# A two-block model on one core: the MLP's down product kept feature-major, and its up product in chunks of 256 columns

## Chip, core and metric

The kernel runs on one core of a Trainium2 chip. The metric is the device time of one execution in microseconds (us), lower is better; for the kernel before, three executions were timed.

## What is computed

Two model blocks run one after the other on 256 tokens of width 1024, in float32: a gated linear attention and a differential attention, each followed by an MLP, then a mixing block of three branches, a cross attention and a third MLP. The change touches the three MLPs, which are all alike:

```python
def rms_norm(x, g):
    y = x * rsqrt(mean(x * x, axis=-1) + EPS)
    return y * g
def sqrelu_mlp(xn, w1, w2):             # xn (256, 1024), w1 (1024, 4096), w2 (4096, 1024)
    return square(relu(xn @ w1)) @ w2
h = h + sqrelu_mlp(rms_norm(h, mlp_norm[layer]), mlp_w1[layer], mlp_w2[layer])
```

## The kernel before, in words

All weights (220 MB) are cut on the host into 420 chunks of 1024 x 128 numbers. Two chunks make a slab of 1 MB, and SyncE streams the 210 slabs through a ring of four buffers, `raw`. Float32 accuracy comes from splitting: ScalarE casts a chunk to `w_hi` (fp32r, `cut_hi`, L959), VectorE subtracts to get `w_lo` (bf16, `cut_lo`, L1505), and both run AHEAD = 3 chunks ahead of TensorE over four slots. The other operand is split the same way into `X.hi`, `X.lo` and `X.bf` (`operand` on ScalarE, L965 to L969; `operand_lo` on VectorE, L1518 and L1520); there are two such sets, XA and XB. Each chunk costs hi x hi, hi x lo and lo x bf.

Most chunks go through `chunk` (L373 to L389). The activations are kept feature-major: 128 features on the partitions, 256 tokens in the free dimension. For each of eight k, the 128x128 square of weights is stationary, and `X.hi` (L382) and `X.lo` (L383) move through, 256 columns each; then eight matmuls of 256 columns take `w_lo` with `X.bf` (L388). All 24 add into one half bank of PSUM; chunks take banks 0 to 3 in turn, and `bank_free` counts the banks given back.

The MLP (`mlp`, one function on each engine) has its own two forms. It works in four hidden groups of 1024; a group is 8 up chunks and 8 down chunks, and the two middle groups are turns of a loop.

- `up_chunk` (L414): `X.hi` and `X.lo` lie beside each other, so one matmul of 512 columns (L422) takes both, eight of them to a whole bank, then eight of 256 columns for the low part (L427). VectorE adds the two halves of the bank (TENSOR_REDUCE, L1574), GpSimd takes max(x, 0) (L2133) and squares it (L2135), and the result is split into XB.
- `down_chunk` (L432): here the activations are stationary and the weights move. A chunk holds two k and four column squares; for each k and each half of the tokens there are two matmuls of 512 columns (L441, L442) and later one for the low part (L451). The sums stand token-major in banks 4 to 7 (`down_sums(t, b)`, token half t, column half b) over all four groups.

Since the norm's factor 1/rms belongs to a token and relu squared is homogeneous of degree two, the MLP multiplies by 1/rms squared at the very end (`rtok2`, one number per token, from `rms_tok`). `stats` has TensorE add up GpSimd's sums of squares (L464 as a row of 256 tokens, L467 as a column); it stands after the first chunk of each stage.

At the end of the last group the sums must be turned. ScalarE copies and scales banks 4 and 5 to SBUF (`to_sbuf`, L1017) after down chunk 3, TensorE transposes 8 squares after down chunk 4 (`turn(0)`, L491), and VectorE adds them to H (`final`, L1558, two feature blocks of 256 at a time: a pair). After the last down chunk the same comes again for banks 6 and 7: one copy by ScalarE, one by VectorE (L1590), `turn(1)`, two adds. Each `final` lets ScalarE build the next stage's operand, VectorE its low part, GpSimd its squares (`sum_squares`, L2108 to L2115), and at last TensorE the next stage's chunk. Between these, ScalarE and VectorE have cuts to make, in the order in which the program is written:

```python
cut_hi(c + 8 + j + AHEAD, o + j + AHEAD)          # ScalarE, down chunk j
if last and X is not None and j in (5, 6):
    final(j - 5)
```

In this document MLP 0 is the one of the first attention block (from 178 us), MLP 1 the second (from 534 us), MLP 2 the last of the program (from 1441 us). Behind MLP 2 there are only the eight output DMAs (L1484), issued by ScalarE as the pairs of H are done.

Of the kernel before, what the change touches and what calls it, by code (L numbers as in the profile page):

```python
# [18 lines left out]
ALU = mybir.AluOpType  # L19
# [35 lines left out]
PAIR_ADDS = TAPS - 1  # L55
HN_K, HN_Q = 2 * DIFF_HEADS, 2 * DIFF_HEADS + 2
# [53 lines left out]
def program(nc, w_d, par_d, con_d, gm_d, x_d, mem_d, band_d, out_d):  # L110
    ctx = ExitStack()
    with ctx:
# [25 lines left out]
        rtok2 = sb("rtok2", [P, NT])  # L138
# [71 lines left out]
        m_sum, m_sq = cut(2, T), cut(2, T)  # L210
        m_tok = cut(NT, D)
# [77 lines left out]
        relu_done, sq_done = sem("relu_done"), sem("sq_done")  # L289
        hn_sq, hn_mm, hn_ln, hn_r, hn_out = [sem("hn_" + n) for n in ("sq", "mm", "ln", "r", "out")]  # L290
        tok_out, turned = sem("tok_out"), sem("turned")
# [25 lines left out]
        def down_sums(t, b):  # L317

            return ps[:, 4 + 2 * b + t, :]
# [50 lines left out]
        def _(pe):  # L370
# [43 lines left out]
            def up_chunk(c, j, build):  # L414

                s, bank = j % HI_SLOTS, j % BANKS
                pe.wait_ge(hi_done, c + 1)
                pe.wait_ge(bank_free, c - BANKS + 1)
                for k in range(KC):
                    if build is not None:  # L420
                        pe.wait_ge(XA.lo_done, KC * build + k + 1)
                    mm(ps[:, bank, :], w_hi[:, s, k], XA.both[:, k].rearrange("p a t -> p (a t)"), start=k == 0, stop=False)  # L422
                pe.wait_ge(lo_done, c + 1)
                for k in range(KC):
                    if build is not None:
                        pe.wait_ge(XA.bf_done, KC * build + k + 1)
                    last = mm(ps[:, bank, 0:T], w_lo[:, s, k], XA.bf[:, k], start=False, stop=k == KC - 1)  # L427
                last.then_inc(gemm_done, 1)

            def down_chunk(c, slot, j, build, first, last):  # L430

                s, b, a = slot % HI_SLOTS, j // 4, j % 4  # L432
                pe.wait_ge(hi_done, c + 1)
                for i in range(2):
                    k = 2 * a + i
                    cols = slice(4 * i, 4 * i + 4)
                    if b == 0:
                        pe.wait_ge(XB.lo_done, KC * build + k + 1)
                    for t in range(NT):
                        at = slice(t * P, (t + 1) * P)  # L440
                        mm(down_sums(t, b), XB.hi[:, k, at], w_hi[:, s, cols], start=first and k == 0, stop=False)  # L441
                        mm(down_sums(t, b), XB.lo[:, k, at], w_hi[:, s, cols], start=False, stop=False)  # L442
                pe.wait_ge(lo_done, c + 1)
                for i in range(2):
                    k = 2 * a + i
                    cols = slice(4 * i, 4 * i + 4)
                    if b == 0:
                        pe.wait_ge(XB.bf_done, KC * build + k + 1)
                    for t in range(NT):
                        at = slice(t * P, (t + 1) * P)  # L450
                        done = mm(down_sums(t, b), XB.bf[:, k, at], w_lo[:, s, cols], start=False, stop=last and k == KC - 1)  # L451
# [27 lines left out]
            def mlp(c0, m, x_build, xb_build0, nu):  # L479
# [3 lines left out]
                def turn(b):  # L483

                    for t in range(NT):
                        pe.wait_ge(tok_out, 4 * m + 2 * b + t + 1)
                    for pair in range(2 * b, 2 * b + 2):
                        for i in range(2):
                            n = 2 * pair + i
                            for t in range(NT):  # L490
                                last = nc.tensor.transpose(ps[:, pair, i * T + t * P:i * T + (t + 1) * P],  # L491
                                                           m_tok[:, t, n * P:(n + 1) * P], ident)
                        last.then_inc(turned, 1)
# [1835 lines left out]
```

## Time and profile before

| what | value |
|---|---|
| times of three executions | 1635.01, 1637.58, 1643.14 us |
| median | 1637.58 us |
| profiled execution, first to last instruction (span) | 1632.4 us |
| profiled execution's own time | not among the times shown |
| TensorE matmul busy | 1454.7 us, 89% |
| TensorE weight load busy | 1186.9 us, 73% |
| VectorE, ScalarE, GpSimd busy | 65%, 54%, 25% |
| mean granted TensorE clock | 0.949 of 2.4 GHz |

A profile row names a line of the kernel, the engine, the operation, and out<-in with the shapes. Matmuls are pipelined: the duration shown for one includes its way through the array, so rows are read by their starts. `x8` means that eight alike are merged, from the start of the first to the end of the last. An idle time in brackets stands before the instruction, with what ended it.

### The profile page before, as it was taken

Reading aid. Unit: us, or ns where it says so; the run is one execution under the profiler, and the core shown is the slowest. Engines: PE = TensorE matmul, PEld = TensorE weight load, DVE = VectorE, ACT = ScalarE, POOL = GpSimd, SP = SyncE. Lnnn points to the kernel's source line nnn. Section 1 sums busy time; section 2 is a strip of 40 time slices with the busy share of each in tenths; the row PEclk is TensorE's granted clock in tenths of the full one; section 3 lists DMA queues with packets and bytes.
Section 4 is the critical chain, followed back from the end, with each engine's and each line's share of the span. In section 5 each row is a group of like instructions: output and inputs, shape, how many; then the busy total and the mean of one; then the engine's idle time right before and its main releaser. Section 6 shows DMA issues by size and latency. Waiting matters only on the chain. (4 is left out here: it accounts for less than half of the span.)

```text
span 1632.4 us, 26380 instructions
## 1 busy us (share of the span) xinstructions
PE 1454.7 (89%) x9598; PEld 1186.9 (73%) x9622; DVE 1056.8 (65%) x1664; ACT 885.6 (54%) x1710; POOL 415.4 (25%) x429
## 2 busy tenths in 40 slices
PE   5987899998988899989978879898898799789998
PEld 5876777766866677769877767778786688577776
DVE  4794666665565666666999755567576665366665
ACT  4443545456455544456988655454565465454443
POOL 3000433341001433244987100004000012043332
PEclk9997999998997899999999999999999899999999
DMA  7330455552821455534444322225343343145551
GB/s 293 109 124 26 143 193 196 190 181 103 183 102 52 158 203 183 203 134 152 155 140 147 136 94 104 85 106 182 117 149 129 114 155 132 50 155 190 198 187 70
DMA packets 35304, 233.54 MB, mean 143 GB/s; under 512 B 3840, under 2 KB 6912, under 8 KB 7936
## 3 DMA queue, kind: packets, MB, share of 16 engines
q1 hardware_dynamic: 30816, 223.75, 38.0%
q10 hardware_dynamic: 3216, 4.19, 1.7%
q0 software_dynamic: 1168, 4.20, 0.9%
q8 instruction: 67, 1.10, 0.3%
q14 instruction: 37, 0.30, 0.1%
HBM read 227.93 MB, written 4.19 MB: 142 GB/s over the span
## 5 line engine op out<-in xcount | busy, mean ns | idle before, releaser
L1505 DVE TENSOR_TENSOR w_lo<-raw,w_hi 128x1024 bf16<-128x1024 f32 x420 | 537.5, 1282 | 286.6 <-ACT w_hi L959 282.9
L959 ACT CAST w_hi<-raw 128x1024 fp32r<-128x1024 f32 x420 | 436.4, 1043 | 239.2 <-PE ps L451 96.6
L382 PE MATMUL ps<-xa_both,w_hi 128*128 128x256 f32 x912 | 240.1, 302 | 30.6 <-ACT w_hi L959 11.8
L383 PE MATMUL ps<-xa_both,w_hi 128*128 128x256 f32 x912 | 225.7, 286 | 0.0
L422 PE MATMUL ps<-xa_both,w_hi 128*128 128x512 f32 x768 | 211.2, 415 | 13.4 <-DVE xa_both L1520 13.4
L382 PEld LDWEIGHTS ps<-xa_both,w_hi 128*128 128x128 f32 x912 | 179.6, 197 | 39.2 <-issue 15.7
L382 PE MATMUL ps<-xb_both,w_hi 128*128 128x256 f32 x704 | 189.1, 307 | 20.0 <-DVE xb_both L1518 11.0
L383 PEld LDWEIGHTS ps<-xa_both,w_hi 128*128 128x128 f32 x912 | 179.9, 197 | 0.4
L383 PE MATMUL ps<-xb_both,w_hi 128*128 128x256 f32 x704 | 175.8, 288 | 0.0
L422 PEld LDWEIGHTS ps<-xa_both,w_hi 128*128 128x128 f32 x768 | 140.8, 193 | 45.9 <-DVE xa_both L1520 17.0
L441 PE MATMUL ps<-w_hi,xb_both 128*128 128x512 f32 x384 | 167.1, 435 | 0.0
L382 PEld LDWEIGHTS ps<-xb_both,w_hi 128*128 128x128 f32 x704 | 139.6, 198 | 32.0 <-issue 18.9
L2133 POOL TENSOR_SCALAR arena<-arena 128x256 f32<-128x256 f32 x96 | 86.2, 897 | 292.3 <-DVE arena L1574 292.3
L442 PE MATMUL ps<-w_hi,xb_both 128*128 128x512 f32 x384 | 150.5, 392 | 0.0
L388 PE MATMUL ps<-xa_bf,w_lo 128*128 128x256 bf16 x912 | 123.1, 279 | 21.3 <-DVE w_lo L1505 21.3
L383 PEld LDWEIGHTS ps<-xb_both,w_hi 128*128 128x128 f32 x704 | 140.4, 199 | 0.4
L2162 POOL TENSOR_TENSOR arena<-arena 128x512 f32<-128x512 f32 x90 | 126.9, 1410 | 49.1 <-ACT arena L1219 38.4
L965 ACT CAST xb_both<-arena 128x256 fp32r<-128x256 f32 x152 | 61.4, 404 | 126.7 <-POOL arena L2135 119.4
L2108 POOL TENSOR_TENSOR sumsq<-H 128x256 f32<-128x256 f32 x7 | 4.3, 612 | 433.9 <-DVE H L1542 404.2
L388 PEld LDWEIGHTS ps<-xa_bf,w_lo 128*128 128x128 bf16 x912 | 81.8, 100 | 37.5 <-DVE w_lo L1505 24.6
L427 PE MATMUL ps<-xa_bf,w_lo 128*128 128x256 bf16 x768 | 103.2, 279 | 0.0
L451 PE MATMUL ps<-w_lo,xb_bf 128*128 128x512 bf16 x360 | 96.2, 381 | 1.4
(291 smaller groups left out, 2354.2 us busy)
## 6 DMA issues: line engine op xcount, KB each, us to landing
raw<-weights SPq DMA_DIRECT2D x210, 1024.0 KB, 4.8
band<-arena ACTq DMA_DIRECT2D x1, 3072.0 KB, 35.5
arena<-band POOLq DMA_DIRECT2D x8, 256.0 KB, 3.2
arena<-gla_masks SPq DMA_DIRECT2D x1, 1088.0 KB, 15.2
H<-x_t SPq DMA_DIRECT2D x1, 1024.0 KB, 4.9
arena<-mem_t POOLq DMA_DIRECT2D x1, 1024.0 KB, 5.2
arena<-band POOLq DMA_DIRECT2D x8, 128.0 KB, 2.7
out_t<-H ACTq DMA_DIRECT2D x8, 128.0 KB, 2.1
```

What stands on the lines that cost most here:

```text
L382: mm(ps[:, bank, 0:T], w_hi[:, s, k], X.hi[:, k], start=k == 0, stop=False)
L383: mm(ps[:, bank, 0:T], w_hi[:, s, k], X.lo[:, k], start=False, stop=False)
L388: last = mm(ps[:, bank, 0:T], w_lo[:, s, k], X.bf[:, k], start=False, stop=k == KC - 1)
L422: mm(ps[:, bank, :], w_hi[:, s, k], XA.both[:, k].rearrange("p a t -> p (a t)"), start=k == 0, stop=False)
L427: last = mm(ps[:, bank, 0:T], w_lo[:, s, k], XA.bf[:, k], start=False, stop=k == KC - 1)
L441: mm(down_sums(t, b), XB.hi[:, k, at], w_hi[:, s, cols], start=first and k == 0, stop=False)
L442: mm(down_sums(t, b), XB.lo[:, k, at], w_hi[:, s, cols], start=False, stop=False)
L451: done = mm(down_sums(t, b), XB.bf[:, k, at], w_lo[:, s, cols], start=False, stop=last and k == KC - 1)
L959: nc.scalar.copy(w_hi[:, j % HI_SLOTS].rearrange("p k n -> p (k n)"), raw[:, j // 2 % RING, j % 2]).then_inc(hi_done, 1)
L1505: TT(w_lo[:, j % HI_SLOTS].rearrange("p k n -> p (k n)"), raw[:, j // 2 % RING, j % 2], w_hi[:, j % HI_SLOTS].rearrange("p k n -> p (k n)" ...
L2133: G.tensor_scalar(m_sq[:, j % 2], m_sum[:, j % 2], 0.0, None, ALU.max).then_inc(relu_done, 1)
L2162: G.tensor_tensor(both, both, c_prod[:, a % PRODUCTS], ALU.add).then_inc(ca["add"], 1)
```

## The change

Both MLP forms become plain feature-major chunks. The up chunks go through `chunk` itself; VectorE's one instruction reads the 256 sums, takes max(x, 0) and multiplies by 1/rms per token (so `rstd` is needed before the first of them, and TensorE's `stats` makes the row in place of the column); GpSimd only squares. In the down chunk the weights are stationary and XB moves, 256 columns each; the eight sums (output blocks n) stand in the halves of banks 4 to 7. `DOWN` orders the squares: four chunks with two k and four n each for k 0 to 3, then four chunks that each finish the two n of a pair. So a pair is complete with down chunks 4, 5, 6 and 7 of the last group, and `final` adds it from PSUM directly. Copies, transposes and their buffers are gone. `bank_free` now counts two for a pair.

```diff
+DOWN = [[(k, n) for k in (j // 2 * 2, j // 2 * 2 + 1) for n in range(j % 2 * 4, j % 2 * 4 + 4)] for j in range(4)]
+DOWN += [[(k, n) for n in (2 * p, 2 * p + 1) for k in range(4, 8)] for p in range(4)]
...
+        def down_sums(n):
+            return ps[:, 4 + n // 2, n % 2 * T:(n % 2 + 1) * T]
+        def down_pair(p):
+            return ps[:, 4 + p, :].rearrange("p (n t) -> p n t", n=2)
...
             def down_chunk(c, slot, j, build, first, last):
-                s, b, a = slot % HI_SLOTS, j // 4, j % 4
+                s, ready = slot % HI_SLOTS, {0: (0, 1), 2: (2, 3), 4: (4, 5, 6, 7)}.get(j, ())
                 pe.wait_ge(hi_done, c + 1)
+                for i, (k, n) in enumerate(DOWN[j]):
+                    if k in ready and n == DOWN[j][0][1]:
+                        pe.wait_ge(XB.lo_done, KC * build + k + 1)
+                    opens = first and k == 0 and n % 2 == 0
+                    mm(down_sums(n), w_hi[:, s, i], XB.hi[:, k], start=opens, stop=False)
+                    mm(down_sums(n), w_hi[:, s, i], XB.lo[:, k], start=False, stop=False)
                 pe.wait_ge(lo_done, c + 1)
+                for i, (k, n) in enumerate(DOWN[j]):
+                    if k in ready and n == DOWN[j][0][1]:
                         pe.wait_ge(XB.bf_done, KC * build + k + 1)
+                    done = mm(down_sums(n), w_lo[:, s, i], XB.bf[:, k], ...)
                 done.then_inc(gemm_done, 1)
...
                     for j in range(8):
-                        up_chunk(c + j, o + j, x_build if first and j == 0 else None)
+                        chunk(c + j, o + j, XA, x_build if first and j == 0 else None)
                         if first and j == 0:
-                            stats(nu, False, True)
+                            stats(nu, True, False)
...
                         down_chunk(c + 8 + j, o + j, j, xb_build0 + g, first, last)
-                        if last and j == 4:
-                            turn(0)
-                    if last:
-                        turn(1)
...
                 def final(pair):                                   # ScalarE
-                    act.wait_ge(bank_free, c0 + 60 + pair + 1)
+                    act.wait_ge(bank_free, c0 + 56 + 2 * pair + 2)
...
                         if first and j == 0:
-                            rms_tok()
+                            rms(nu, rstd)
...
-                        if last and j == 4:
-                            act.wait_ge(gemm_done, c + 12)
-                            for t in range(NT):
-                                to_sbuf(t, 0)
                         cut_hi(c + 8 + j + AHEAD, o + j + AHEAD)
-                        if last and X is not None and j in (5, 6):
+                        if last and X is not None and j >= 5:
                             final(j - 5)
-                    if last:
-                        act.wait_ge(gemm_done, c + 16)
-                        to_sbuf(0, 1)
-                        if X is not None:
-                            final(2)
-                            final(3)
+                    if last and X is not None:
+                        final(3)
...
                 def final(pair):                                   # VectorE
-                    dve.wait_ge(turned, 4 * m + pair + 1)
-                    TT(H[:, 2 * pair:2 * pair + 2], ps[:, pair, :].rearrange("p (n t) -> p n t", n=2), H[:, 2 * pair:2 * pair + 2],
-                       ALU.add).then_inc(bank_free, 1)
+                    dve.wait_ge(gemm_done, c0 + 60 + pair + 1)
+                    h = H[:, 2 * pair:2 * pair + 2]
+                    TT(h, down_pair(pair), h, ALU.add).then_inc(bank_free, 2)
...
-                        V.tensor_reduce(m_sum[:, j % 2], ps[:, (o + j) % BANKS, :].rearrange("p (a t) -> p t a", a=2), AX.X,
-                                        ALU.add).then_inc(bank_free, 1 if j < 7 else 5 if last else 9)
+                        if first and j == 0:
+                            dve.wait_ge(rstd_done, nu + 1)
+                        STT(m_relu[:, j % 2], got(c + j, o + j), 0.0, rstd[:], ALU.max, ALU.mult).then_inc(bank_free, 9 if j == 7 and not last else 1)
...
-                        if last and j == 5:
-                            final(0)
-                            final(1)
-                        if last and X is not None and j in (6, 7):
+                        if last and j >= 5:
+                            final(j - 5)
+                        if last and X is not None and j >= 6:
                             final_lo(j - 6)
                     if last:
-                        dve.wait_ge(gemm_done, c + 16)
-                        dve.wait_ge(tok_out, 4 * m + 3)
-                        TS(m_tok[:, 1, 512:1024], down_sums(1, 1), rtok2[:, 1:2], None, ALU.mult).then_inc(tok_out, 1)
-                        for pair in (2, 3):
-                            final(pair)
+                        final(3)
...
-                        G.tensor_scalar(m_sq[:, j % 2], m_sum[:, j % 2], 0.0, None, ALU.max).then_inc(relu_done, 1)
-                        pool.wait_ge(relu_done, 32 * m + 8 * g + j + 1)
-                        G.tensor_tensor(m_sq[:, j % 2], m_sq[:, j % 2], m_sq[:, j % 2], ALU.mult).then_inc(sq_done, 1)
+                        G.tensor_tensor(m_sq[:, j % 2], m_relu[:, j % 2], m_relu[:, j % 2], ALU.mult).then_inc(sq_done, 1)
```

How the order moves at two places. First VectorE at the end of MLP 0, from the cut that goes with down chunk 5 on. Before (L1505 is the weight cut, L1558 the add of a pair to H, L1520 the low part of the next operand, L1590 the copy for the transposes):

```order
L1505 TENSOR_TENSOR w_lo<-raw,w_hi 128x1024 [waits hi_done] x5
L1558 TENSOR_TENSOR H<-ps,H 128x512 [waits turned] x2
L1505 TENSOR_TENSOR w_lo<-raw,w_hi 128x1024 [waits hi_done]
L1520 SCALAR_TENSOR_TENSOR xa_both<-H,par,xa_both 128x256 [waits xa_hi_done] x2
L1505 TENSOR_TENSOR w_lo<-raw,w_hi 128x1024 [waits hi_done]
L1520 SCALAR_TENSOR_TENSOR xa_both<-H,par,xa_both 128x256 [waits xa_hi_done] x2
L1590 TENSOR_SCALAR arena<-ps,rtok 128x512 [waits tok_out,gemm_done]
L1558 TENSOR_TENSOR H<-ps,H 128x512 [waits turned] x2
L1520 SCALAR_TENSOR_TENSOR xa_both<-H,par,xa_both 128x256 [waits xa_hi_done] x4
```

In the changed kernel the same place reads as follows (L1452 is the cut, L1506 the add, L1467 the low part):

```order
L1452 TENSOR_TENSOR w_lo<-raw,w_hi 128x1024 [waits hi_done] x5
L1506 TENSOR_TENSOR H<-ps,H 128x512 [waits gemm_done]
L1452 TENSOR_TENSOR w_lo<-raw,w_hi 128x1024 [waits hi_done]
L1506 TENSOR_TENSOR H<-ps,H 128x512 [waits gemm_done]
L1467 SCALAR_TENSOR_TENSOR xa_both<-H,par,xa_both 128x256 [waits xa_hi_done] x2
L1452 TENSOR_TENSOR w_lo<-raw,w_hi 128x1024 [waits hi_done]
L1506 TENSOR_TENSOR H<-ps,H 128x512 [waits gemm_done]
L1467 SCALAR_TENSOR_TENSOR xa_both<-H,par,xa_both 128x256 [waits xa_hi_done] x2
L1506 TENSOR_TENSOR H<-ps,H 128x512 [waits gemm_done]
L1467 SCALAR_TENSOR_TENSOR xa_both<-H,par,xa_both 128x256 [waits xa_hi_done] x4
```

The adds of the second and third pair each moved behind one more cut; the copy is gone.

Second TensorE, where down chunk 4 of the last group of MLP 0 ends and chunk 5 begins, before:

```order
L451 MATMUL ps<-w_lo,xb_bf 128x512 [waits lo_done]
L451 MATMUL ps<-w_lo,xb_bf 128x512 x3
L491 MATMUL ps<-con,arena 128x128 [waits tok_out]
L491 MATMUL ps<-con,arena 128x128 x7
L441 MATMUL ps<-w_hi,xb_both 128x512 [waits hi_done]
```

And in the changed kernel (L425 and L426 are the new down chunk's matmuls with `XB.hi` and `XB.lo`, L431 those of the low part):

```order
L431 MATMUL ps<-xb_bf,w_lo 128x256 [waits lo_done]
L431 MATMUL ps<-xb_bf,w_lo 128x256 x7
L425 MATMUL ps<-xb_both,w_hi 128x256 [waits hi_done]
L426 MATMUL ps<-xb_both,w_hi 128x256
L425 MATMUL ps<-xb_both,w_hi 128x256
```

The eight transposes and their wait for ScalarE's copies are gone, and eight low matmuls of 256 columns stand where four of 512 stood.

## Rows read from the trace of the kernel before

**Rows 1.** Cores: span and mean clock.

```profile
core 0: 1632.4 us, clock 0.949
```

**Rows 2.** Windows, one loop turn of MLP 0: stretch, length, busy (count), clock, DMA.

```profile
229.66:273.40 43.74, 43.62 (x223) 31.57 (x224) 28.16 (x33) 21.60 (x32) 14.77 (x16) 1.00 0.56 193
```

**Rows 3.** Chain of waits in MLP 2: start, us, what.

```profile
1454.80 1.87 PE ps L422 x8
1456.67 0.89 PE ps L427 x8
1457.56 1.88 PE ps L422 x8
...
1493.07 1.85 PE ps L422 x8
...
1536.85 1.85 PE ps L422 x8
...
1580.63 1.85 PE ps L422 x8
```

**Rows 4.** Timeline, TensorE, plain chunks: start, us, engine, line, operation.

```profile
752.54 1.05 PE L388 MATMUL ps<-xa_bf,w_lo 128*128 128x256 bf16 x8
...
782.46 1.05 PE L388 MATMUL ps<-xa_bf,w_lo 128*128 128x256 bf16 x8
```

**Rows 5.** Timeline, all engines, the end of MLP 0.

```profile
347.44 0.58 PE L441 MATMUL ps<-w_hi,xb_both 128*128 128x512 f32 x1
...
350.15 0.58 PE L441 MATMUL ps<-w_hi,xb_both 128*128 128x512 f32 x1
...
353.06 1.04 PE L491 MATMUL ps<-con,arena 128*128 128x128 f32 x8
353.31 1.05 ACT L959 CAST w_hi<-raw 128x1024 fp32r<-128x1024 f32 x1 [0.57 <-PE ps L451]
...
353.85 0.48 PE L441 MATMUL ps<-w_hi,xb_both 128*128 128x512 f32 x1
...
354.40 1.22 DVE L1505 TENSOR_TENSOR w_lo<-raw,w_hi 128x1024 bf16<-128x1024 f32 x1 [0.40 <-ACT w_hi L959]
...
355.54 1.28 DVE L1558 TENSOR_TENSOR H<-ps,H 128x512 f32<-128x512 f32 x2
...
356.26 0.51 ACT L968 ACTIVATE xa_both<-H,par 128x256 fp32r<-128x256 f32 x1 [1.89 <-DVE H L1558]
...
357.47 0.49 ACT L969 ACTIVATE xa_bf<-H,par 128x256 bf16<-128x256 f32 x1
...
361.26 1.04 PE L451 MATMUL ps<-w_lo,xb_bf 128*128 128x512 bf16 x4
...
365.23 1.07 PE L491 MATMUL ps<-con,arena 128*128 128x128 f32 x8 [2.94 <-DVE arena L1590]
...
366.67 0.61 POOL L2112 TENSOR_TENSOR sqtmp<-H 128x256 f32<-128x256 f32 x1 [4.12 <-DVE H L1558]
...
372.33 0.79 POOL L2115 TENSOR_TENSOR sumsq<-sumsq,sqtmp 128x256 f32<-128x256 f32 x1
...
373.17 1.22 PE L464 MATMUL ps<-sumsq,ones 128*128 128x256 f32 x2 [0.81 <-POOL sumsq L2115]
...
374.18 0.85 PE L467 MATMUL ps<-ones,sumsq 128*128 128x1 f32 x4
...
374.89 0.56 PE L382 MATMUL ps<-xa_both,w_hi 128*128 128x256 f32 x1
```

**Rows 6.** Timeline, the end of MLP 1.

```profile
718.64 1.04 PE L451 MATMUL ps<-w_lo,xb_bf 128*128 128x512 bf16 x4
...
730.85 1.22 PE L464 MATMUL ps<-sumsq,ones 128*128 128x256 f32 x2
```

**Rows 7.** Timeline, the end of the program.

```profile
1624.32 1.04 PE L451 MATMUL ps<-w_lo,xb_bf 128*128 128x512 bf16 x4
...
1627.75 1.29 DVE L1558 TENSOR_TENSOR H<-ps,H 128x512 f32<-128x512 f32 x2 [0.81 <-PE ps L491]
```

More of the change, by code:

```diff
@@ L209, in program @@
         cut = Cut()
-        m_sum, m_sq = cut(2, T), cut(2, T)
-        m_tok = cut(NT, D)
+        m_relu, m_sq = cut(2, T), cut(2, T)
         cut = Cut(1024)
@@ L412, in token_half, with down_chunk @@
                     last.then_inc(gemm_done, 2)
-            def up_chunk(c, j, build):
-                s, bank = j % HI_SLOTS, j % BANKS
+            def down_chunk(c, slot, j, build, first, last):
+                s, ready = slot % HI_SLOTS, {0: (0, 1), 2: (2, 3), 4: (4, 5, 6, 7)}.get(j, ())
                 pe.wait_ge(hi_done, c + 1)
[L418 to L422, printed above, removed]
-                pe.wait_ge(lo_done, c + 1)
[L424 to L428, printed above, removed]
@@ L430, in down_chunk @@
-            def down_chunk(c, slot, j, build, first, last):
-                s, b, a = slot % HI_SLOTS, j // 4, j % 4
[L433 to L438, printed above, removed]
-                    for t in range(NT):
[L440 to L447, printed above, removed]
+                for i, (k, n) in enumerate(DOWN[j]):
[4 more added lines that the diff above has]
+                    mm(down_sums(n), w_hi[:, s, i], XB.lo[:, k], start=False, stop=False)
@@ L448, in down_chunk @@
+                pe.wait_ge(lo_done, c + 1)
+                for i, (k, n) in enumerate(DOWN[j]):
+                    if k in ready and n == DOWN[j][0][1]:
                         pe.wait_ge(XB.bf_done, KC * build + k + 1)
-                    for t in range(NT):
-                        at = slice(t * P, (t + 1) * P)
-                        done = mm(down_sums(t, b), XB.bf[:, k, at], w_lo[:, s, cols], start=False, stop=last and k == KC - 1)
+                    done = mm(down_sums(n), w_lo[:, s, i], XB.bf[:, k], start=False, stop=last and (k, n) == DOWN[j][-1] and j >= 4)
@@ L481, in mlp @@
                 o = c0 % 8
[L483 to L493, printed above, removed]
                 def group(g, first, last):
@@ L1482, in _ @@
             for n in range(KC):
-                act.wait_ge(bank_free, C_M2 + 60 + n // 2 + 1)
+                act.wait_ge(bank_free, C_M2 + 56 + n // 2 * 2 + 2)
                 act.dma_start(out_d[:, n], H[:, n]).then_inc(out_done, 16)
@@ L2234, in squares @@
     def squares(w):
-        w = np.asarray(w).reshape(4, 2, P, 2, 4, P)
-        return [w[a, :, :, b].transpose(0, 2, 1, 3).reshape(D, P) for b in range(2) for a in range(4)]
+        w = np.asarray(w).reshape(KC, P, KC, P)
+        return [np.concatenate([w[k, :, n] for k, n in order]) for order in DOWN]
     def mlp(w1, w2):
```

16 lines of the change are left out of this document (2 added, 14 removed).

## Prediction

> **What bounds the kernel now.** I read the clock and span first [rows 1], then the windows over one group of an MLP, the chain of waits in MLP 2, and the timelines where MLPs end. In one turn of the MLP loop TensorE is busy for 43.62 of 43.74 us at a granted clock of 1.00, the 2.4 GHz level; VectorE has 28.2 us of work in it, ScalarE 21.6, GpSimd 14.8, and the DMA engines are busy at 0.56 [rows 2]. The chain agrees: through the groups it is TensorE alone, one chunk behind the other [rows 3]. So inside a group only the pace of the matmuls counts. A saving on VectorE or GpSimd there is worth nothing: TensorE's work covers it, and would still cover it if VectorE had 10 us more in a group. At the ends of MLP 0 and 1 it is otherwise: TensorE waits 2.94 us for VectorE's copy before `turn(1)`, and later for GpSimd's last sum of squares [rows 5]. Behind MLP 2 everything lies on the path.
>
> **Pace inside the groups.** An up chunk takes 1457.56 - 1454.80 = 2.76 us, and a whole group 1536.85 - 1493.07 = 43.78 us, the next one the same [rows 3]. A down chunk takes 350.15 - 347.44 = 2.71 us [rows 5]. The plain chunk, whose form both now take, goes from 752.54 to 782.46 in 11 chunks, 2.720 us each, at full clock [rows 4]. Columns are equal in all three (8 x 512 + 8 x 256, 12 x 512, 24 x 256: 6144), so the change swaps few long matmuls for many short ones at nearly the same price. A group becomes 16 x 2.720 = 43.52 us, 0.26 less; 12 groups give **3.1 us**. The bounds of this term: the up saving alone, 96 x 0.04 = 3.8 us, above; below, see the first rival. The weight layout within a chunk changes, its bytes do not, so the DMAs stay. Waits for XB stand in down chunks 0, 2 and 4 now, not in 0 to 3: the last parts are needed one chunk later, at nothing.
>
> **Start of an MLP.** `stats` makes the row (L464, 374.18 - 373.17 = 1.01 us) in place of the column (L467, 374.89 - 374.18 = 0.71) [rows 5], with TensorE waiting for it in line: 3 x 0.3, **0.9 us lost**. VectorE's first read of PSUM now waits for `rstd`, some 1.5 us longer (row sum, then two ScalarE instructions of 256). Behind it on VectorE stand a cut for chunk 4 and the next read. TensorE has chunks 1 to 3 cut and banks for them, 3 x 2.7 us: hidden. If that cover were gone it would cost those 1.5 us three times.
>
> **End of MLP 0.** I count from the end of down chunk 4, 350.15 + 2.71 = 352.86. ScalarE sees it at 353.31, 0.45 later; its cut lets VectorE's cut start at 354.40 and the add to H at 355.54; ScalarE's casts start at 356.26 and end by 357.96 [rows 5]. `turn(0)` kept chunk 5 back from 352.86 to 353.85: 0.99 us.
> After the change each pair takes the whole round in turn, as the second listing of VectorE's order shows: cut, cut, add, four casts, 1.09 + 1.14 + 0.72 + 1.61 = 4.56 us (1.61, since the next cut follows at once). The down chunks come every 2.72 us, so this round, not TensorE, paces the pairs. The first starts at 0.45; the third, at 0.45 + 2 x 4.56 = 9.57, has its add from 11.80 to 12.50. Only then are enough banks back for the next stage's first chunk, though the sums of that pair are ready at about 5.9. TensorE is idle from 8.2 to 12.5, longer than now. But what the next stage really waits for is GpSimd: four squares and sums from 366.67 to 373.12, 6.45 us, then `stats` at 373.17, which is 20.31 after my zero [rows 5]. From 12.55 the same four end at 19.0 (the last pair's add, at about 14, is in time for the third), `stats` at 19.05. By an estimate from the same rounds the low parts end at 16.1 and chunk 0's low matmuls by 18.3, before that. Gain **1.3 us**. The bounds: nothing, if VectorE's adds slip behind its low parts; 4.1 us (0.99 + the 3.1 of copies and transposes), if the round were no limit. I take the worked value.
> **End of MLP 1**: its last chunk's low matmuls start at 718.64, so zero is 718.64 - (361.26 - 352.86) = 710.24, and `stats` at 730.85 is 20.61 after it [rows 5, 6]. To 19.05: **1.6 us**.
>
> **End of MLP 2.** ScalarE has no cuts left, so the pairs are added as they come. The last low matmuls end at 1624.32 + 1.04 = 1625.36; the adds of pairs 2 and 3 end at 1629.04 [rows 7], and the span 3.36 later with the last output DMAs. Now one add of 0.65 follows the matmuls, and two DMAs as before it: 4.05 us in place of 7.04, and `turn(0)`'s 0.99 too. **4.0 us**. Bounds 3 and 4.5, by how the DMAs queue.
>
> **Sum**: 3.1 - 0.9 + 1.3 + 1.6 + 4.0 = 9.1 us. From the span of 1632.4 that is 1623.3. The median of the runs is 5.2 above this span; the profiled execution's own time is not shown, and I take the same distance: 1637.6 - 9.1 = **1628.5 us**.
>
> **Rivals.**
> *Short matmuls cost more in the new down chunk (slower).* The plain chunk adds all 24 matmuls into one half bank with the same stationary square twice in a row. The down chunk changes the half bank after every two, in the low part after every one, which no row shows for 256 columns. Price: its 12 long matmuls take 2.71 us where 6144 columns at 2.4 GHz are 2.56, an excess of 0.15 for 12. Were that excess per matmul, 24 would pay 0.30: 0.15 more per chunk, 96 x 0.15 = 14.4 us, 1643 us, slower than before. It decides from 9.1 us / (96 x 24) = 3.9 ns per matmul on, and passes 0.5% slower at 7.5 ns. Against it: the 512-column form changes its bank after every two as well, and keeps an even 2.71; and the plain chunk pays nothing for being short. Chance 0.1.
> The Trainium skill (TensorE: Matmul & The Clock Gate, "Back-to-back issue gap") gives 81 ns per matmul at 128 columns and 131 at 512 in a sustained stream, so long ones would be far cheaper per column; by an estimate between these, 98 ns at 256, the change would cost 8 x (196 - 131) ns more per up chunk and 12 x 65 ns per down chunk, about 125 us in all. The trace does not agree: its 512-column matmuls follow each other at 1.87 / 8 = 234 ns, its 256-column ones at 2.720 / 24 = 113 [rows 3, 4].
>
> *The ends give nothing.* The new rounds of cut, add and casts could take longer than mine, with GpSimd and VectorE slowing each other; TensorE's longer idle could leave a slower clock for the next chunk. Then 9.1 - 2.9 = 6.2, 1631.4 us. For it: 4.56 is one undisturbed round. Against: GpSimd's start moves with the third add alone. Chance 0.18.
>
> *The pace does not move*: the up chunk's 0.04 us is taken back in the down chunk. 9.1 - 3.1 = 6.0, 1631.6 us. Chance 0.15. In one sense the change then does not do what it says: only the transposes go.
>
> *More than worked out*: the ends give their upper bound, 1628.5 - 5.3 = 1623.2. Chance 0.07.
>
> **How the numbers follow.** The forecast has 0.5, with its own range 1626 to 1631. The range for 8 in 10 is 1623 to 1639: it takes in the second to the fourth rival and the low end of the first, plus some scatter between runs, which shows 1635 to 1643 for one kernel. A measurement tells about 0.5% from no change, 8.2 us: the line is at 1629.4. Faster by more: most of the forecast's half and the last rival, 0.45. Within: the rest of it, the two middle rivals and over half of the first, 0.49. Slower by more: 0.06.
>
> **What would show it.** Right: groups of 43.5 us in all MLPs; down chunks at 2.72; no copy or transpose rows; VectorE's pair adds about 4.6 us apart at the ends of MLP 0 and 1; `stats` 19 us after down chunk 4; 4 us from the last matmul to the end; TensorE's weight loads much busier in the MLPs at the same pace. Wrong: a down chunk at 2.8 us or more; idle TensorE within a group; pair adds 5 us or more apart, or TensorE at the lower clock (1.2 GHz) for longer behind the MLPs.

## The result, and the profile after

The changed kernel is slower: 1644.55 us median of 20 runs (1639.69 to 1648.86), against 1638.22 of 20 runs of the kernel before on the same chips (1634.44 to 1644.94). The ratio is 1.0033, with a 95% interval of 1.0021 to 1.0045: 5.4 us more, where 9.1 us less were forecast, and outside the range. The profiled execution is the longest of the 20, 1648.86 us, with a span of 1647.1, 14.7 over [rows 1]; so the spans of the two profiles differ by more than the kernels do.

From the page of the kernel after, the busy time and share of each engine (with the number of instructions):

```profile
PE 1476.1 (90%) x11488; PEld 1329.0 (81%) x11488; DVE 1031.3 (63%) x1661; ACT 892.6 (54%) x1701; POOL 307.8 (19%) x333
```

Its windows, a stretch inside the groups of MLP 0, with the columns of [rows 2]:

```profile
230.00:274.50 44.50, 44.50 (x384) 42.56 (x383) 25.85 (x33) 22.55 (x32) 5.68 (x8) 1.00 0.53 190
```

TensorE is never idle and at full clock there, as before, and its weight loads are now busy for 42.56 of 44.50 us. VectorE and GpSimd have less to do than before (25.85 against 28.16 us, 5.68 against 14.77); ScalarE, with the same 32 instructions, is busy for 22.55 against 21.60. So the path inside a group is still TensorE's alone. But the chain of waits in MLP 2 shows a slower one, against 2.76 and 43.78 in [rows 3] (start, us, engine; the low part of an up chunk is L391, that of a down chunk L431):

```profile
1511.27 0.89 PE ps L391 x8
1514.06 0.89 PE ps L391 x8
...
1533.61 0.89 PE ps L431 x8
...
1555.96 0.89 PE ps L391 x8
```

An up chunk takes 1514.06 - 1511.27 = 2.79 us, a down chunk (1555.96 - 1533.61) / 8 = 2.79, a group 1555.96 - 1511.27 = 44.69, where 43.52 was forecast. The surprise stands in the plain chunks between the MLPs, which the diff does not touch. TensorE's timeline at the place of [rows 4]:

```profile
752.64 1.05 PE L391 MATMUL ps<-xa_bf,w_lo 128*128 128x256 bf16 x8
...
753.65 0.28 PE L386 MATMUL ps<-xa_both,w_hi 128*128 128x256 f32 x1
...
755.31 0.28 PE L386 MATMUL ps<-xa_both,w_hi 128*128 128x256 f32 x1
...
783.23 1.05 PE L391 MATMUL ps<-xa_bf,w_lo 128*128 128x256 bf16 x8
```

Eleven of them take 783.23 - 752.64 = 30.59 us, 2.781 each, where [rows 4] have 2.720. Within a chunk the matmuls of the high part follow each other at (755.31 - 753.65) / 14 = 119 ns. The low part (`X.bf` and `w_lo`, bf16) keeps its 0.89 us [rows 3]. So something made the 256-column matmuls of the high part slower: by the pitch of the chunks it is 0.061 / 16 = 4 ns for each in the plain chunks and 0.073 / 16 = 5 ns in the MLPs. The granted clock is 1.00 in both places, as before, so it is not the clock.

The end of MLP 0, from ScalarE's cut that follows down chunk 4 (all engines, with [rows 5]):

```profile
359.22 1.05 ACT L923 CAST w_hi<-raw 128x1024 fp32r<-128x1024 f32 x1 [1.80 <-PE ps L431]
...
361.44 0.68 DVE L1506 TENSOR_TENSOR H<-ps,H 128x512 f32<-128x512 f32 x1
...
365.98 0.68 DVE L1506 TENSOR_TENSOR H<-ps,H 128x512 f32<-128x512 f32 x1
...
370.95 0.68 DVE L1506 TENSOR_TENSOR H<-ps,H 128x512 f32<-128x512 f32 x1
...
378.51 0.87 PE L444 MATMUL ps<-sumsq,ones 128*128 128x256 f32 x2
```

The prediction puts the cut 0.45 us after down chunk 4's end, which gives 358.77 for the zero of its count, and the three pair adds that matter are 4.54 and 4.97 us apart. `stats` follows 378.51 - 358.77 = 19.7 us after zero. The end of the program, with [rows 7]:

```profile
1642.39 1.05 PE L431 MATMUL ps<-xb_bf,w_lo 128*128 128x256 bf16 x8
```

The last low matmuls end at 1642.39 + 1.05 = 1643.44, the span at 1647.1: 3.7 us in place of 7.04. The end of the program brought what it should, the end of MLP 0 under half of it (`stats` 19.7 us after zero, against 20.31 before and 19.05 in the forecast); the pace took it all back and more.

### The profile page after: what moved, and what is told of

It reads as the page before. It is cut to its first block and busy times, and to the rows that moved or that the text cites. A ratio compares the mean times of both kernels' runs of the same rounds, so it can differ in the third digit from the quotient of the medians.

```text
span 1647.1 us, 30014 instructions
## 1 busy us (share of the span) xinstructions
PE 1476.1 (90%) x11488; PEld 1329.0 (81%) x11488; DVE 1031.3 (63%) x1661; ACT 892.6 (54%) x1701; POOL 307.8 (19%) x333
## 5 line engine op out<-in xcount | busy, mean ns | idle before, releaser
L1452 DVE TENSOR_TENSOR w_lo<-raw,w_hi 128x1024 bf16<-128x1024 f32 x420 | 535.1, 1274 | 306.0 <-ACT w_hi L923 302.5
L385 PE MATMUL ps<-xa_both,w_hi 128*128 128x256 f32 x1680 | 445.1, 301 | 47.5 <-DVE xa_both L1467 16.7
L386 PE MATMUL ps<-xa_both,w_hi 128*128 128x256 f32 x1680 | 420.6, 287 | 0.0
L385 PEld LDWEIGHTS ps<-xa_both,w_hi 128*128 128x128 f32 x1680 | 327.3, 195 | 60.3 <-issue 24.3
L386 PEld LDWEIGHTS ps<-xa_both,w_hi 128*128 128x128 f32 x1680 | 328.8, 196 | 0.6
L391 PE MATMUL ps<-xa_bf,w_lo 128*128 128x256 bf16 x1680 | 227.9, 280 | 20.2 <-DVE w_lo L1452 20.2
L385 PE MATMUL ps<-xb_both,w_hi 128*128 128x256 f32 x704 | 193.8, 310 | 18.6 <-DVE xb_both L1465 10.5
L425 PE MATMUL ps<-xb_both,w_hi 128*128 128x256 f32 x768 | 194.8, 292 | 0.0
L391 PEld LDWEIGHTS ps<-xa_bf,w_lo 128*128 128x128 bf16 x1680 | 151.0, 100 | 49.7 <-DVE w_lo L1452 23.7
L426 PE MATMUL ps<-xb_both,w_hi 128*128 128x256 f32 x768 | 186.7, 281 | 0.0
L386 PE MATMUL ps<-xb_both,w_hi 128*128 128x256 f32 x704 | 180.9, 292 | 0.0
L385 PEld LDWEIGHTS ps<-xb_both,w_hi 128*128 128x128 f32 x704 | 140.4, 199 | 30.3 <-issue 18.4
L425 PEld LDWEIGHTS ps<-xb_both,w_hi 128*128 128x128 f32 x768 | 145.2, 189 | 1.1
L426 PEld LDWEIGHTS ps<-xb_both,w_hi 128*128 128x128 f32 x768 | 145.7, 190 | 0.0
L2075 POOL TENSOR_TENSOR arena<-arena 128x256 f32<-128x256 f32 x96 | 68.2, 711 | 406.2 <-DVE arena L1522 406.2
L386 PEld LDWEIGHTS ps<-xb_both,w_hi 128*128 128x128 f32 x704 | 141.4, 201 | 0.3
L431 PE MATMUL ps<-xb_bf,w_lo 128*128 128x256 bf16 x768 | 100.7, 274 | 0.0
L391 PE MATMUL ps<-xb_bf,w_lo 128*128 128x256 bf16 x704 | 97.4, 284 | 0.0
L1166 ACT ACTIVATE arena<-arena,par 128x256 f32<-128x256 f32 x180 | 77.6, 496 | 6.6 <-POOL arena L2102 6.6
```

The costliest lines, as they stand in the source:

```text
L385: mm(ps[:, bank, 0:T], w_hi[:, s, k], X.hi[:, k], start=k == 0, stop=False)
L386: mm(ps[:, bank, 0:T], w_hi[:, s, k], X.lo[:, k], start=False, stop=False)
L391: last = mm(ps[:, bank, 0:T], w_lo[:, s, k], X.bf[:, k], start=False, stop=k == KC - 1)
L425: mm(down_sums(n), w_hi[:, s, i], XB.hi[:, k], start=opens, stop=False)
L426: mm(down_sums(n), w_hi[:, s, i], XB.lo[:, k], start=False, stop=False)
L431: done = mm(down_sums(n), w_lo[:, s, i], XB.bf[:, k], start=False, stop=last and (k, n) == DOWN[j][-1] and j >= 4)
```

## The experiments

Two theories for the pace stood at first. **Layout**: the diff also deletes the tile `rtok2` (8 bytes per partition). On-chip tiles are laid out in the order of their `sb` calls, and each starts at a multiple of 32 bytes, so that a tile of 8 bytes can push the next by 32. (This is how the program is built; the traces show no addresses, and all distances below are worked out from that rule and the tiles' sizes.) So everything behind `rtok2` (`hn_sqb`, `hn_rb`, `gains`, the arena, `XA`, `XB`) starts 32 bytes earlier, while `w_hi`, `w_lo`, `H` and the others that stand ahead stay. **Form**: something in the new code (the down chunk's change of half bank, the doubled traffic of weight loads) slows TensorE. That untouched chunks are slower too speaks for the first. Each experiment is compared with the kernel before, in the same session. Diffs are against the changed kernel unless said.

**1. Put 8 unused bytes where `rtok2` was.**

```diff
         rtok_mem = sb("rtok_mem", [P, NT])
+        spare = sb("spare", [P, NT])
         hn_sqb = sb("hn_sqb", [P, 2, T])
```

> The changed kernel with an unused tile of 8 bytes per partition where rtok2 stood, so that hn_sqb, hn_rb, gains, the arena, XA, XB and the small operands start at their old addresses again (multiples of 64 bytes; in the changed kernel they all start 32 bytes past one). Address theory: the fp32r matmuls of 256 columns go from 119 ns apart back to 113, every plain chunk and every MLP chunk from 2.79 to 2.72 us, an MLP group from 44.7 to 43.5, and the time lands where the forecast had it, 1626 to 1632 us, a ratio to before of 0.992 to 0.996. Form theory (the new MLP chunks, or the program's denser stream of weight loads, cost more by themselves): chunks stay at 2.79 and the time at 1642 to 1647, ratio 1.003.

Measured: 1627.76 us against 1640.21, ratio 0.9929 (0.99 to 0.9957), span 1626.2. No instruction differs from the changed kernel's but for the addresses; lines are one higher. Timeline of TensorE (plain chunks), chain (MLP 2), and windows:

```profile
751.90 1.05 PE L392 MATMUL ps<-xa_bf,w_lo 128*128 128x256 bf16 x8
...
752.91 0.28 PE L387 MATMUL ps<-xa_both,w_hi 128*128 128x256 f32 x1
...
754.51 0.28 PE L387 MATMUL ps<-xa_both,w_hi 128*128 128x256 f32 x1
...
781.82 1.05 PE L392 MATMUL ps<-xa_bf,w_lo 128*128 128x256 bf16 x8
```

```profile
1493.83 0.89 PE ps L392 x8
...
1537.35 0.89 PE ps L392 x8
```

```profile
230.00:340.00 110.00, 110.00 (x973) 105.50 (x971) 67.49 (x86) 58.98 (x86) 16.31 (x23) 1.00 0.55 193
```

Chunks are back at (781.82 - 751.90) / 11 = 2.720 us, matmuls at (754.51 - 752.91) / 14 = 114 ns, and a group takes 43.52 us, the forecast to the hundredth. The weight loads are busy for 105.50 of 110 us at this pace too, so their traffic is not what slowed the changed kernel. An unused tile of 8 bytes is worth 1.0033 - 0.9929 = 1.0% of the program.

**2. The opposite: the kernel before, with `rtok2` allocated last.** All its code stays.

```diff
-        rtok2 = sb("rtok2", [P, NT])
...
         XA, XB = XSet("xa"), XSet("xb")
+        rtok2 = sb("rtok2", [P, NT])
```

> The kernel before, with rtok2 allocated last instead of ahead of hn_sqb: no instruction changes, XA, XB and the arena start 32 bytes past a multiple of 64. Address theory: plain chunks slow down from 2.72 to 2.78 us although the MLP form is the old one; what the 512-column matmuls do is open: in the up chunk XA moves, so 8 x 6 ns more if the cost is per matmul, twice that if it is per column; in the down chunk XB is stationary and the weights (not moved) stream, so nothing. Time 1645 to 1655, ratio 1.004 to 1.010. Form theory: nothing changes, ratio 0.998 to 1.002.

Measured: 1643.56 us, ratio 1.002 (1.0005 to 1.0034). TensorE's timeline (plain chunks), then the chain in MLP 2 (L451 is the low part of the old down chunk, L427 of the old up chunk):

```profile
753.57 1.05 PE L388 MATMUL ps<-xa_bf,w_lo 128*128 128x256 bf16 x8
...
781.37 1.05 PE L388 MATMUL ps<-xa_bf,w_lo 128*128 128x256 bf16 x8
```

```profile
1504.99 0.89 PE ps L427 x8
...
1524.31 0.89 PE ps L427 x8
1529.82 0.88 PE ps L451 x4
1532.56 0.88 PE ps L451 x4
```

The plain chunk goes to 27.80 / 10 = 2.78 us, without any of the new code: layout alone does it. The old up chunk, 512 columns wide, stays at 19.32 / 7 = 2.76, and the old down chunk goes from 2.71 to 2.74. So the direction was right and the size too large (a ratio of 1.004 or more was expected), and between the two old forms it came the other way round: the up chunk, where `XA` moves, pays nothing, and the down chunk, where `XB` is stationary, pays 0.03 us. The old MLP forms hardly feel the shift. That is also why the changed kernel pays more for it than the kernel before would: the change turned 192 chunks of insensitive forms into the sensitive one.

**3 and 4. Which of the shifted tiles?** In experiment 3 the only spare 8 bytes stand behind the arena, so that the arena and what is ahead of it stay shifted while `XA` and `XB` are back in place; in 4 there is a spare in `rtok2`'s place as well, so that only `XA` and `XB` (and the small tiles behind them) are off, now by +32.

The diff is that of 4; 3 has only the second tile.

```diff
         rtok_mem = sb("rtok_mem", [P, NT])
+        spare = sb("spare", [P, NT])
         hn_sqb = sb("hn_sqb", [P, 2, T])
...
         arena = sb("arena", [P, ARENA])
+        spare_x = sb("spare_x", [P, NT])
```

> The changed kernel with the 8 unused bytes behind the arena instead: the arena, hn_sqb, hn_rb and gains stay 32 bytes off, XA, XB and the small operands are back on multiples of 64. If TensorE's fp32r operand is what counts: as e1, within 0.2 percent, chunks 2.72 us. If it is the arena's traffic (VectorE, ScalarE, GpSimd, the attention matmuls): as the changed kernel, 1.003, chunks 2.79.

> The changed kernel with both spare tiles: the arena and what lies before it are back on multiples of 64, XA, XB and the small operands alone are 32 bytes off. The mirror of e3. If TensorE's operand counts: as the changed kernel, chunks 2.79 us, ratio 1.002 to 1.004. If the arena counts: as e1.

Measured: experiment 3, 1632.26 us, 0.9953 (0.9933 to 0.9973), chunks at 2.72; experiment 4, 1642.28, 1.0017 (1.0003 to 1.003), chunks at 2.78. Plain chunks of experiment 4:

```profile
752.73 1.05 PE L393 MATMUL ps<-xa_bf,w_lo 128*128 128x256 bf16 x8
...
777.75 1.05 PE L393 MATMUL ps<-xa_bf,w_lo 128*128 128x256 bf16 x8
```

25.02 / 9 = 2.78 us. The place of `XA` and `XB`, the operands that stream through TensorE, sets the pace. Experiment 3 is 4.5 us above experiment 1 at the same pace of the chunks; the granted clock of their runs differs (see below).

**5 and 6. Which places are good?** In 5 each `X.both` is a view that begins 16 bytes into a tile 64 bytes longer, so `XA` starts 16 bytes and `XB` 80 bytes behind its old place. In 6 both start 64 bytes behind theirs (diff against 4). The theory under test in 6 was that a boundary of 64 bytes decides.

```diff
-        spare_x = sb("spare_x", [P, NT])
+        spare_x = sb("spare_x", [P, 16])
```

> As e1, but XA.both and XB.both (hi and lo) start 16 bytes past a multiple of 64 in place of 0 (the bf16 sets stay on multiples of 64). Theory 1, a row of 1024 bytes that doesn't start on a 64-byte line costs a line more: as the changed kernel, plain chunks at 2.78 us, ratio to before 1.001 to 1.004. Theory 2, only an odd multiple of 32 costs (two halves of a line in the wrong order): as e1, 2.72 us, ratio 0.992 to 0.996.

> As e1, but XA and XB start 64 bytes later: on a multiple of 128, where they stood 64 past one. If 64 bytes is the size that counts: as e1 within 0.15 percent, chunks 2.72 us. If it is 128 or more and e1 is only less bad than the changed kernel: chunks faster than 2.72 (down to 2.66), time 1612 to 1622.

Measured: 5, 1643.98 us, 1.0042 (1.0026 to 1.0059); 6, 1645.49 us, 1.005 (1.0035 to 1.0064). Plain chunks of experiment 6:

```profile
754.05 1.05 PE L393 MATMUL ps<-xa_bf,w_lo 128*128 128x256 bf16 x8
...
781.98 1.05 PE L393 MATMUL ps<-xa_bf,w_lo 128*128 128x256 bf16 x8
```

27.93 / 10 = 2.79 us: a shift by 64 is as bad as one by 32, and that theory fell. In experiment 5 `XA`'s chunks take 2.78 to 2.80 us, but `XB`'s have two paces. Chain in MLP 2, down chunks of the first group and of the second:

```profile
1484.25 0.89 PE ps L433 x8
...
1503.24 0.89 PE ps L433 x8
...
1528.32 0.89 PE ps L433 x8
...
1547.83 0.89 PE ps L433 x8
```

The first group goes at 18.99 / 7 = 2.71, the second at 19.51 / 7 = 2.79. This is no scatter: in all three MLPs the first group has 2.71 and the other three 2.76 to 2.80, with nearly the same order of the values in each. So at this place something else than the layout decides as well, and the first groups are even a little faster than 2.72.

**9, 10, 11. Absolute place, or distance to the weights?** 9 shifts `w_hi` and everything behind it by 64 bytes, so all distances stay. 10 shifts `w_hi` by 64 and `XA`, `XB` by 128. 11 shifts `XA` and `XB` alone by 128. (Diffs against experiment 1; 10 has both lines.)

```diff
         raw = sb("raw", [P, RING, 2, D])
+        spare_w = sb("spare_w", [P, 16])
         w_hi = sb("w_hi", [P, HI_SLOTS, KC, P], F32R)
...
         arena = sb("arena", [P, ARENA])
+        spare_x = sb("spare_x", [P, 16])
```

> As e1, with 64 unused bytes ahead of w_hi, so that w_hi, w_lo and everything behind them start 64 bytes later: weights 64 past a multiple of 128, XA and XB on one (in e1 weights 0, X 64; in e6, slow, weights 0, X 0). Theory of the distance: what counts is where the streamed operand starts against the weights that are loaded beside it, modulo 128; the distance is 64 as in e1, so chunks 2.72 us and ratio 0.991 to 0.996. Theory of X's own address: X at 0 modulo 128 is slow as in e6, chunks 2.79, ratio 1.002 to 1.006.

> As e9, with 64 more bytes ahead of XA: weights at 64, X at 64 modulo 128, distance 0. Distance theory: slow as e6, chunks 2.79 us, ratio 1.002 to 1.006. Theory of X's own address: fast as e1 (X at 64), 2.72, ratio 0.991 to 0.996.

> As e1, with XA and XB 128 bytes later, 192 modulo 256 where e1 has 64; weights as in e1. If the pattern repeats every 128 bytes: as e1, 2.72 us, ratio 0.991 to 0.996. If it repeats over a longer stretch: chunks between 2.72 and 2.79, ratio up to 1.006.

Measured: 9, 1627.8 us, 0.9917 (0.9891 to 0.9943), chunks at 2.72; 10, 1645.56, 1.0029 (1.0015 to 1.0043), 2.79; 11, 1646.19, 1.0037 (1.002 to 1.0055), 2.77. Plain chunks of experiment 9:

```profile
752.54 1.05 PE L393 MATMUL ps<-xa_bf,w_lo 128*128 128x256 bf16 x8
...
779.74 1.05 PE L393 MATMUL ps<-xa_bf,w_lo 128*128 128x256 bf16 x8
```

27.20 / 10 = 2.72 us. In 9 `XA` starts 64 bytes behind its place in the kernel before, exactly as in 6, and the pace is good, where in 6 it was bad. What counts is a distance, not the place: the one between the streamed operand and the weights, or strictly one to some tile that moved with the weights, since `H` and the small tiles up to `rtok_mem` did too. Experiment 11 shows that the pattern does not repeat after 128 bytes.

**12, 13, 14. The other distances.** One run each, with different gaps ahead of `XA` and between `XA` and `XB`, so that one kernel tries two distances; what is compared is `XA` with `XB` inside a run. Their diffs have the form of 11's, with 64, 112 and 80 floats ahead of `XA` and 32, 56 and 48 between.

> As e1, XA at distance 448 and XB at distance 64 from w_hi, modulo 512 (e1: 192 and 192, chunks 2.72; slow so far: 160, 208, 224, 256, 320, chunks 2.77 to 2.79). Read from the profile, XA's and XB's chunks apart. If the pattern repeats every 256 bytes: XA's chunks 2.72, XB's 2.77. If every 512 or more: both 2.77 to 2.79, or XB's something new.

> As e1, XA at distance 128, XB at 352 modulo 512. No theory names these as fast: 2.77 to 2.79 for both if 192 is a narrow spot; near 2.72 for one of them if there are several.

> As e1, XA at distance 0, XB at 192 modulo 512 and modulo 1024 (e1: 704 modulo 1024). If the pattern repeats every 256 or 512 bytes: XB's chunks 2.72, and XA's 2.79 as in e6. If it is longer than 512: both slow.

Measured: 1632.43, 1643.94 and 1637.27 us, against 1640.18 for one run of the kernel before. Chain in MLP 2 of experiment 12 (L395: up chunks, which stream `XA`; L435: down chunks, `XB`):

```profile
1496.94 0.89 PE ps L395 x8
...
1515.98 0.89 PE ps L395 x8
1518.76 0.89 PE ps L435 x8
...
1538.17 0.89 PE ps L435 x8
```

and of experiment 14:

```profile
1501.41 0.89 PE ps L395 x8
...
1520.96 0.89 PE ps L395 x8
1523.69 0.89 PE ps L435 x8
...
1542.73 0.89 PE ps L435 x8
```

In 12 `XA` goes at 19.04 / 7 = 2.72 and `XB` at 19.41 / 7 = 2.77; in 14 it is the other way round, `XA` at 19.55 / 7 = 2.79 and `XB` at 19.04 / 7 = 2.72. Both are slow in 13. The operand whose distance fits is fast in the same run in which the other is slow. That the pattern repeats after 256 bytes was one of the outcomes named ahead of 12 and 14, and it came. All of it in one table (distance of `X.both`'s start from `w_hi`'s start, in bytes per partition, its remainder by 256; pitch of a chunk in us):

| remainder | kernels | pitch |
|---|---|---|
| 0 | 6 and 10 (both operands), `XA` of 14 | 2.79 to 2.80 |
| 16 | `XB` of 5 | 2.71 in the first group of each MLP, 2.76 to 2.80 in the others |
| 64 | 11 (both), `XB` of 12 | 2.77 to 2.78 |
| 96 | `XB` of 13 | 2.80 |
| 128 | `XA` of 13 | 2.77 to 2.81 |
| 160 | the changed kernel, plain chunks of 2 | 2.77 to 2.80 |
| 192 | plain chunks of before, 1, 3, 9, `XA` of 12, `XB` of 14 | 2.72 |
| 208 | `XA` of 5 | 2.78 to 2.80 |
| 224 | 4 (both) | 2.78 |

**8. The swap of forms by itself.** Experiment 1 with the old up chunk of 512 columns put back. VectorE still makes one eviction of 256 columns, so this kernel leaves out of the up sums the product of the weights' high part with the operand's low part.

```diff
-                        chunk(c + j, o + j, XA, x_build if first and j == 0 else None)
+                        up_chunk(c + j, o + j, x_build if first and j == 0 else None)
```

> As e1, with the up chunks in their old form: eight matmuls of 512 columns over hi and lo, eight of 256. VectorE reads the first half of the bank only, so the output leaves out the hi x lo part of the up product. Everything else is e1. By the prediction's term the old up form is 0.04 us per chunk slower: MLP groups 43.8 against 43.5, 96 x 0.04 = 3.6 us above e1, ratio 0.995 to 0.998. If the form itself makes no difference: as e1.

Measured: 1632.47 us, 0.9965 (0.995 to 0.9979), span 1632.3. Chain in MLP 2 (L426: the old up matmuls):

```profile
1497.15 1.87 PE ps L426 x8
...
1516.47 1.87 PE ps L426 x8
```

An up chunk takes (1516.47 - 1497.15) / 7 = 2.76 us, against 2.72 in experiment 1. Over 96 up chunks that is 3.8 us, and the difference of the ratios, 0.0036 or 5.9 us, holds it within the intervals. At the good distance the short matmuls are indeed cheaper than the old up form. The old down form was not put back by itself: its 2.71 us stand against 2.72 in experiment 1.

**7. The end of an MLP, improved.** In experiment 1 VectorE's order puts the weight cut ahead of the add of a pair, and the cut waits for a cut of ScalarE that is itself queued behind the casts of the pair before. Here the add comes first (against experiment 1, in the last group's down chunks).

```diff
+                        if last and j >= 5:
+                            final(j - 5)
                         cut_lo(c + 8 + j + AHEAD, o + j + AHEAD)
                         if j == 0:
                             operand_lo(XB, n0 + 8, 7, m_sq[:, 1])
-                        if last and j >= 5:
-                            final(j - 5)
```

> As e1, with VectorE's add of a pair to H ahead of its weight cut in down chunks 5 to 7 of the last group, where it stood behind it. In e1 the adds of MLP 0 come at 357.00, 361.54 and 366.51, paced by cut, cut, add and casts in turn, and stats starts 19.8 us after down chunk 4. Theory: the add no longer waits for ScalarE's cut, ScalarE's round is 1.04 + 1.61 us and fits under a down chunk, the adds come 2.7 us apart, TensorE idles under 1 us, and stats starts 14 to 15 us after down chunk 4, then paced by GpSimd's squares. 4 to 5 us at each end of MLP 0 and 1: 8 to 10 us below e1, ratio 0.987 to 0.990. Rival (the stages behind give it back, or GpSimd's chain is the real limit): 0 to 3 us below e1.

Measured: 1621.53 us against 1637.85, ratio 0.9905 (0.9889 to 0.9921), span 1619.4. The end of MLP 0 in experiment 1:

```profile
354.77 1.05 ACT L924 CAST w_hi<-raw 128x1024 fp32r<-128x1024 f32 x1 [1.73 <-PE ps L432]
...
357.00 0.68 DVE L1507 TENSOR_TENSOR H<-ps,H 128x512 f32<-128x512 f32 x1
...
361.54 0.68 DVE L1507 TENSOR_TENSOR H<-ps,H 128x512 f32<-128x512 f32 x1
...
366.51 0.68 DVE L1507 TENSOR_TENSOR H<-ps,H 128x512 f32<-128x512 f32 x1
...
367.29 0.55 PE L386 MATMUL ps<-xa_both,w_hi 128*128 128x256 f32 x1 [4.45 <-DVE H L1507]
...
374.08 1.11 PE L445 MATMUL ps<-sumsq,ones 128*128 128x256 f32 x2
```

and in experiment 7:

```profile
355.16 1.05 ACT L924 CAST w_hi<-raw 128x1024 fp32r<-128x1024 f32 x1 [1.73 <-PE ps L432]
355.18 0.69 DVE L1507 TENSOR_TENSOR H<-ps,H 128x512 f32<-128x512 f32 x1 [0.49 <-PE ps L432]
...
361.70 0.68 DVE L1507 TENSOR_TENSOR H<-ps,H 128x512 f32<-128x512 f32 x1
...
362.98 0.37 PE L386 MATMUL ps<-xa_both,w_hi 128*128 128x256 f32 x1
...
370.87 1.11 PE L445 MATMUL ps<-sumsq,ones 128*128 128x256 f32 x2
```

Zero is 354.32 and 354.71. The third add starts 12.2 us after zero in the one and 7.0 in the other; TensorE, idle for 4.45 us in the one, goes straight on at 362.98 in the other, and waits only 0.25 to 0.73 us at a time inside the chunk. `stats` comes 19.8 and 16.2 us after zero, 3.6 us gained, and at the end of MLP 1 the start of `stats` moves from 726.53 to 719.33. GpSimd's last sum ends at 370.72, just ahead of `stats`, and keeps the rest. So the profiles give 7.2 us for both ends, under the 8 to 10 that were expected; `stats` was expected 14 to 15 us after zero. The spans differ by 6.8 and the ratios by 0.0024, 3.9 us, with intervals that overlap. This kernel beats both: 1% below the kernel before, 1.3% below the changed one.

## Why the prediction was wrong

**The step that failed** is in "Pace inside the groups": "The plain chunk, whose form both now take, goes ... 2.720 us each", taken as the price of a group, and with it the unsaid premise that an instruction that the diff leaves alone keeps its duration. 2.720 is the price of that form at one distance of `XA` from `w_hi`, 192 modulo 256 bytes, and the deleted tile made it 160. The forecast had read the diff for what it issues and not for what it allocates. `rtok2` was in it, in plain sight. The price: 44.69 - 43.52 = 1.17 us for a group, 14.0 for the twelve, and 0.06 in a plain chunk; the conv stretch between MLP 1 and MLP 2 shows 4.6 us (`stats` to `stats` 422.9 us, 418.3 in experiment 1). All told the spans of the changed kernel and experiment 1 differ by 20.9 us, with the changed kernel's span that of its longest run; the ratios differ by 1.04%, 17 us.

With the tile put back, the other steps can be read in experiment 1:

- **Pace, 3.1 us**: right. Groups of 43.52 us; experiment 8 confirms the up half of the swap on its own.
- **Stats row for column, 0.9 us lost**: wrong, it costs nothing. The 1.01 us of [rows 5] goes from the row's start to that of the column's matmuls, which no longer follow. Nor is the start of the next chunk's first matmul the measure: it comes 0.50 us after the row's in experiment 1 (MLP 0, 189.55 to 190.05) and 0.72 after the column's in the kernel before (187.16 to 187.88), both at a granted clock of 0.50, the 1.2 GHz level, but behind the row that first matmul holds up the second. Counted to the second one, less one undisturbed pitch at that clock, the row takes 190.63 - 189.55 - 0.21 = 0.87 us and the column 188.45 - 187.16 - 0.43 = 0.86. VectorE's later first read was hidden, as said: TensorE is never idle in the 40 us behind `stats`.
- **End of MLP 0, 1.3 us; of MLP 1, 1.6**: mechanism right, size too large. `stats` came 19.8 us after zero at both, not 19.05, so 0.5 and 0.8. The first round of a pair took 4.54 us (4.56 forecast), the second 4.97, because VectorE's cut took 1.66 in place of 1.23 (GpSimd's squares ran at that time; that they are the reason was not tested); and the four squares took 6.66 in place of 6.45.
- **End of MLP 2, 4.0 us**: right, a little low. From the last low matmuls' end to the span's 3.6 us (4.05 forecast), and the 0.99 of `turn(0)`: 4.4.
- **DMAs, VectorE and GpSimd at nothing**: right.

Sum: 3.1 + 0.5 + 0.8 + 4.4 = 8.8 us, where 9.1 was forecast. That the two are so near is partly luck: a loss of 0.9 that was none and a gain 0.4 too small stand against 1.6 too much at the ends of MLP 0 and 1. Experiment 1 measures 1% to 0.43% of 1640, 7 to 16 us, with 11.6 in the middle.

**A term that neither the forecast nor this sum has** is the granted clock, the mean over a run. It goes with the time: of the changed kernel's 20 runs the shortest (1639.69 us) had 0.949, the six above 1647 us had 0.942 to 0.944, and on average 0.001 less goes with 1.1 us more. The mean over the runs is 0.945 for the changed kernel, 0.946 for experiment 1, 0.943 for experiment 3 and 0.949 for the kernel before in the session of the two experiments. By that estimate some 4 us of the changed kernel's time and 3 of experiment 1's are the clock's, and most of experiment 3's distance from experiment 1. Why the kernels differ in it was not tested. The paces above were all read at a granted clock of 1.00, so this does not touch them.

**The rivals.** The slower one named 1643 us, near what came, and its signs nearly came too: a down chunk at 2.79 us ("2.8 us or more"), 0.073 / 24 = 3.0 ns per matmul (3.9). But its mechanism, a price for changing the half bank or for many short matmuls, is not what happened: up chunks and untouched chunks paid too, and with the layout restored the same instructions take 2.72. The number alone would have confirmed a wrong story. "The pace does not move" is out by the groups of experiment 1 and by experiment 8; "the ends give nothing" by experiment 1, though the ends of MLP 0 and 1 gave less than half of their 2.9 us. No rival named the layout.

**What stays open.** Which part of the chip makes the distance matter (the reading of the weights and of the streamed operand from the same memory is the obvious suspect; no run here shows it). Whether `w_lo`, `H` or the small tiles, which always moved with `w_hi`, have a share. Why at remainder 16 the first group of an MLP goes at 2.71 and the others do not. Whether other remainders than the nine tried are good, and whether other kernels' good place is 192 too. Why the 512-column form of the up chunk doesn't feel it: it loads weights half as often per column, but that was not tested by itself.

## What to carry to other kernels

Compare the start addresses of on-chip tiles before and after an edit, as one compares instructions: a deleted 8-byte tile cost 1% of this program and turned a gain of 0.7% into a loss of 0.3%. If chunks that an edit did not touch change their pace, suspect the layout first, and put the old layout back with an unused tile before judging the edit. And take an instruction's price from a row in which the same instruction follows it as will in the new place, and read it to where the rhythm behind it is the usual one again. Put each run's granted clock beside its time.

## What was not expected of the hardware

- A 256-column matmul of the 4-byte type, weights loaded anew for each, follows the last at 114 ns when `X.both` starts 192 bytes (modulo 256) behind `w_hi`, and at 118 to 120 at seven of the eight other remainders tried; at 16 it is 114 in the first group of an MLP and up to 119 in the others. 208 and 224 on one side and 160 on the other are slow already (176 was not tried); the pattern repeats after 256 bytes as far as tried (remainders by 512 of 192 and 448 are both fast).
- The low part (bf16, 0.89 us for 8) does not change with the distance. The old up form with its 512-column matmuls (2.76 us a chunk) is the same at the remainders 192 and 160, the only ones at which it ran; the old down form, with the activations stationary, loses 0.03 us a chunk between them.
- Weight loads busy for 96% of a stretch (105.50 of 110 us) do not slow the matmuls: in the kernel before they are at 72% in a group [rows 2], at nearly the same pace per column. The Trainium skill (TensorE: Matmul & The Clock Gate, "Back-to-back issue gap") would have long matmuls far cheaper per column than short ones. The traces do not agree: for the same 6144 columns the short form takes 2.72 us, the two old ones 2.76 and 2.71.
